# Retention weights split early into two stored parts, and small products on two column tiles

## What is computed

```python
def ab_mixer(...):
    ql, kl, vl, gl, ul = jnp.split(h_lat @ w_in, cuts, axis=-1)   # retention q, k, v, gate; S5 input
    qc, kc, vc, gc, uc = jnp.split(h_ctx @ w_in, cuts, axis=-1)
    r_l, r_c = retention_mixer(...)     # bidirectional retention, 4 heads of 128
    s_l, s_c = s5_mixer(...)            # bidirectional diagonal state space, 32 groups of 16 channels
    y_l = jnp.concatenate([r_l, s_l], axis=-1) @ w_out
```

## Time and profile before

| | |
|---|---|
| Time, median of 3 runs | 1839.15 us (1837.81 to 1839.74) |
| The profiled execution | 1839.42 us, its span 1837.6 us |
| PE busy | 1773.7 us, 97% of the span |
| DVE busy | 1194.3 us, 65% |
| ACT busy | 726.1 us, 40% |
| Moved by DMA | 257.81 MB, 140 GB/s in the mean |
| Granted TensorE clock, mean | 0.987 |

### The profile page before, as it was taken

How to read it: one execution, slowest core, us unless ns; L and a number is a source line. 1 busy time by engine, 2 the same in 40 slices (tenths; PEclk the granted TensorE clock), 3 DMA queues, 4 the chain that set the end, 5 groups by cost and what they waited for, 6 DMA issues and landing times.

```text
span 1837.6 us, 25748 instructions
## 1 busy us (share of the span) xinstructions
PE 1773.7 (97%) x9970; PEld 1516.5 (83%) x9970; DVE 1194.3 (65%) x1890; ACT 726.1 (40%) x1027; POOL 62.2 (3%) x41
## 2 busy tenths in 40 slices
PE   7999999999989799999999999999999999999998
PEld 5788888888787588888888888888888898689997
DVE  4677677778999655876677367766433534855554
ACT  4422122336888734322222242222222433854343
POOL 0000000020000010000000100000002000010001
PEclk8999999999999899999999999999999999999999
DMA  8444454332110122554454335544222342035543
GB/s 333 184 184 154 170 225 183 131 114 74 56 36 35 46 92 100 198 186 163 170 213 147 105 138 190 187 154 177 93 87 96 137 183 69 1 131 183 188 176 124
DMA packets 40440, 257.81 MB, mean 140 GB/s; under 512 B 4752, under 2 KB 6032, under 8 KB 15536
## 3 DMA queue, kind: packets, MB, share of 16 engines
q1 hardware_dynamic: 40368, 256.86, 38.4%
HBM read 255.79 MB, written 1.05 MB: 140 GB/s over the span
## 4 chain that ended last, share of the span: by engine, by line
PE 82%; DVE 10%; ACT 5%; issue 2%; DMA 1%; POOL 0%; ACTq 0%; SPq 0%; DVEq 0%; POOLq 0%
PE ps_all L1796 25%; PE ps_all L1800 25%; PE ps_all L1797 25%; DVE w_lo L1048 2%; ACT w_hi L568 2%; DVE sq_acc L1526 1%; PE ps_all L1792 1%; PE banks L2359 1%; PE banks L2172 1%; PE ps_all L2336 1%; DVE normed L1535 0%; PE ps_all L2159 0%; DVE scaled L1517 0%; DVE wb L1490 0%; PE banks L1891 0%
## 5 line engine op out<-in xcount | busy, mean ns | idle before, releaser
L1796 PE MATMUL ps_all<-a_hi,w_lo 128*128 128x512 f32 (+1 forms) x1832 | 650.9, 355 | 5.0 <-DVE gated L1086 1.6
L1800 PE MATMUL ps_all<-a_lo,w_hi 128*128 128x512 f32 (+1 forms) x1832 | 646.8, 353 | 2.1 <-DVE a_lo L1202 1.2
L1797 PE MATMUL ps_all<-a_hi,w_hi 128*128 128x512 f32 (+1 forms) x1832 | 645.7, 352 | 0.0
L1048 DVE TENSOR_TENSOR w_lo<-w_raw,w_hi 128x2048 fp32r<-128x2048 f32 (+2 forms) x179 | 365.0, 2039 | 149.6 <-ACT w_hi L568 149.4
L568 ACT ACTIVATE w_hi<-w_raw 128x2048 fp32r<-128x2048 f32 (+2 forms) x179 | 306.1, 1710 | 318.3 <-PE ps_all L1800 307.6
L1796 PEld LDWEIGHTS ps_all<-a_hi,w_lo 128*128 128x128 f32 x1832 | 345.9, 189 | 56.2 <-DVE w_lo L1048 4.2
L1800 PEld LDWEIGHTS ps_all<-a_lo,w_hi 128*128 128x128 f32 x1832 | 345.9, 189 | 51.5 <-DVE a_lo L1202 2.7
L1797 PEld LDWEIGHTS ps_all<-a_hi,w_hi 128*128 128x128 f32 x1832 | 346.0, 189 | 47.1 <-issue 0.2
L1060 DVE SCALAR_TENSOR_TENSOR mod_junk<-mod_raw,cond 128x1024 bf16<-128x1024 f32 x256 | 302.7, 1220 | 7.7 <-ACT cond L596 5.4
L1796 PE MATMUL ps_all<-g_hi,w_lo 128*128 128x512 f32 (+1 forms) x734 | 261.2, 356 | 1.5 <-DVE w_lo L1048 1.5
L1797 PE MATMUL ps_all<-g_hi,w_hi 128*128 128x512 f32 (+1 forms) x734 | 259.3, 353 | 0.0
(11 more groups left out here) (280 smaller groups left out, 1526.4 us busy)
## 6 DMA issues: line engine op xcount, KB each, us to landing
w_raw<-in_tiles SPq DMA_DIRECT2D x118, 1024.0 KB, 4.8
mod_raw<-in_w_mod SPq DMA_DIRECT2D x64, 1024.0 KB, 4.8
w_raw<-in_tiles SPq DMA_DIRECT2D x32, 768.0 KB, 4.1
w_raw<-in_tiles SPq DMA_DIRECT2D x32, 640.0 KB, 3.8
start_w<-in_w_start SPq DMA_DIRECT2D x8, 1024.0 KB, 19.3
bias<-in_na_bias SPq DMA_DIRECT2D x2, 1536.0 KB, 9.2
h<-in_h SPq DMA_DIRECT2D x4, 512.0 KB, 7.0
cond<-in_cond SPq DMA_DIRECT2D x2, 1024.0 KB, 18.0
```

Of the source, the lines that this page charges most:

```text
L1048: nc.vector.tensor_tensor(w_lo[:, slot, 0:size], w_raw[:, slot, 0:size], w_hi[:, slot, 0:size].bitcast(F32), ALU.subtract).then_inc(lo_rea ...
L1796: pe.matmul(dst, w[1], x[0], start=start, stop=False)
L1797: pe.matmul(dst, w[0], x[0], start=False, stop=False)
L1800: return pe.matmul(dst, w[0], x[1], start=False, stop=stop_)
```

## The change

The retention tiles are no longer split in the mixer. A new input `split` holds them as 16 pieces of 128 x 1024. In `ffn0.up0` from tile 2 on, and in the first six tiles of `ffn0.down0`, SP loads one piece per tile, ACT rounds it (`piece_to_high`, behind silu and `g_hi`), DVE subtracts (`piece_to_low`, behind gating or residual), and SP stores both parts in a tensor `parts` in device memory. Round 1 of `ffn0.up0` is taken out of the loop on SP, ACT and DVE. In the mixer SP loads `parts` straight into `w_hi` and `w_lo` (`fetch_parts`), and PE waits for `parts_in` in place of `lo_ready`. The glu tiles are loaded earlier, and semaphore counts are adapted. The kernel products of both pairs of a round are issued alternately on two column tiles (PSUM partitions 0 to 31 and 32 to 63).

```diff
+        def piece_at(segment, it, slot):
+
+            if segment == "ffn0.up0" and not early(it, 1):
+                return 2 * it + slot - 2
+            if segment == "ffn0.down0" and not (isinstance(it, int) and it == 3):
+                return 2 * it + slot + 10
+            return None
+
+        piece_raw = scaled[:].rearrange("p s t -> p (s t)")
+        piece_high = normed[:].rearrange("p s t -> p (s t)").bitcast(F32R)
+        piece_low = sq[:].rearrange("p s t -> p (s t)").bitcast(F32R)
...
+            def store_piece(p):
+
+                sp.wait_ge(piece_hi, p + 1)
+                sp.dma_start(parts[bass.ds(p, 1), 0].rearrange("a p c -> (a p) c"), piece_high.bitcast(F32)).then_inc(piece_stored, 16)
+                sp.wait_ge(piece_lo, p + 1)
+                sp.dma_start(parts[bass.ds(p, 1), 1].rearrange("a p c -> (a p) c"), piece_low.bitcast(F32)).then_inc(piece_stored, 16)
+
+            def load_piece(p):
+
+                if early(p, 1):
+                    sp.wait_ge(a_ready, KT)
+                src = i["split"][bass.ds(p, 1)].rearrange("a p c -> (a p) c")
+                sp.dma_start(piece_raw, src).then_inc(piece_in, 16)
+
+            def fetch_parts(j):
+
+                sp.wait_ge(pe_done, BASE["ret_in"] + j - 1)
+                sp.dma_start(w_hi[:, j % 2].bitcast(F32).rearrange("p (a c) -> p a c", a=2),
+                             parts[2 * j:2 * j + 2, 0].rearrange("a p c -> p a c")).then_inc(parts_in[j % 2], 16)
+                sp.dma_start(w_lo[:, j % 2].bitcast(F32).rearrange("p (a c) -> p a c", a=2),
+                             parts[2 * j:2 * j + 2, 1].rearrange("a p c -> p a c")).then_inc(parts_in[j % 2], 16)
+
+            def retention_input():
+
+                for j in range(1, 8):
+                    fetch_parts(j)
+                    if j <= 2:
+                        sp.wait_ge(lo_ready, BASE["ret_in"])
+                        sp.dma_start(w_raw[:, j - 1, 0:width("glu")], i["tiles"][BASE["glu"] + j - 1, :, 0:width("glu")]
+                                     ).then_inc(w_in[j - 1], 16)
+
             def body(segment, it, last):
 
                 for slot in range(2):
                     n = BASE[segment] + 2 * it + slot
+                    if segment == "s5_in" and slot == 1:
+                        sp.wait_ge(piece_stored, 32 * PIECES)
+                        fetch_parts(0)
+                        continue
+                    if segment == "glu" and slot == 0:
+                        continue
                     if early(n, 1):
...
                     fetch_mod(segment, it, slot)
+                    p = piece_at(segment, it, slot)
+                    if p is not None:
+                        if not early(p, 1):
+                            store_piece(p - 1)
+                        load_piece(p)
+                    elif segment == "ffn0.down0" and slot == 0:
+                        store_piece(PIECES - 1)
...
+                if segment == "ffn0.up0":
+                    body(segment, 1, False)
                 if its > 2:
-                    with sp.Fori(1, its - 1) as it:
+                    with sp.Fori(2 if segment == "ffn0.up0" else 1, its - 1) as it:
                         body(segment, it, False)
...
+            def piece_to_high(p):
+
+                if p is not None:
+                    act.wait_ge(piece_in, 16 * (p + 1))
+                    if early(p, 1):
+                        act.wait_ge(a_ready, KT)
+                    else:
+                        act.wait_ge(piece_stored, 32 * p)
+                    nc.scalar.activation(piece_high, piece_raw, ACT.Copy).then_inc(piece_hi, 1)
...
                         finish(it, slot)
+                        piece_to_high(piece_at(segment, it, slot))
...
-                split_hi(base + 1, 2048, 1)
...
-                    split_hi(base + b + 2, 2048 if b < 6 else width("glu"), b % 2)
+                    if b >= 6:
+                        passed[0] = 64
+                        split_hi(base + b + 2, width("glu"), b % 2, 9 if b == 6 else 1)
...
+            def piece_to_low(p):
+
+                if p is not None:
+                    dve.wait_ge(piece_hi, p + 1)
+                    if not early(p, 1):
+                        dve.wait_ge(piece_stored, 32 * p)
+                    nc.vector.tensor_tensor(piece_low, piece_raw, piece_high.bitcast(F32), ALU.subtract).then_inc(piece_lo, 1)
...
                         gating(it, slot)
+                        piece_to_low(piece_at(segment, it, slot))
...
-                    if b < 7:
-                        split_lo(base + b + 2, 2048 if b < 6 else width("glu"), b % 2)
+                    if b == 6:
+                        split_lo(base + 8, width("glu"), 0, 9)
...
-                        pe.wait_ge(lo_ready, n + 1)
+                        pe.wait_ge(parts_in[slot], 32 * (j // 2 + 1))
...
-                def kernel_products(pair):
-
-                    b, ql = pair // 2, pair % 2
-                    at = 224 * ql
+                def kernel_products(b):
+
                     pe.wait_ge(S["c"], b + 1)
                     pe.wait_ge(S["present"], b + 1)
                     if b:
                         pe.wait_ge(S["k"], 2 * b)
-                    c = [cp[:, b % 2, ql, ri] for ri in range(2)]
-                    fwd = [wb[:, 2 * ql, ri, 3, :] for ri in range(2)]
-                    bwd = [wb[:, 2 * ql + 1, ri, 0, :] for ri in range(2)]
+                    c = [[cp[:, b % 2, ql, ri] for ri in range(2)] for ql in range(2)]
+                    fwd = [[wb[:, 2 * ql, ri, 3, :] for ri in range(2)] for ql in range(2)]
+                    bwd = [[wb[:, 2 * ql + 1, ri, 0, :] for ri in range(2)] for ql in range(2)]
+                    to = [ps_sum[32 * ql:32 * ql + 32] for ql in range(2)]
                     for ri in range(2):
-                        pe.matmul(ps_sum[0:32, at:at + 96], bwd[ri], state_rows(c[ri][:, 6:9]), start=(ri == 0), stop=(ri == 1))
-                    pe.matmul(ps_sum[0:32, at + 96:at + 224], fwd[0], state_rows(c[0][:, 0:4]), start=True, stop=False)
-                    pe.matmul(ps_sum[0:32, at + 96:at + 224], fwd[1], state_rows(c[1][:, 0:4]), start=False, stop=False)
+                        for ql in range(2):
+                            pe.matmul(to[ql][:, 0:96], bwd[ql][ri], state_rows(c[ql][ri][:, 6:9]), start=(ri == 0), stop=(ri == 1))
                     for ri in range(2):
-                        pe.matmul(ps_sum[0:32, at + 96:at + 128], bwd[ri], c[ri][:, 9, :], start=False, stop=False)
-                    pe.matmul(ps_sum[0:32, at + 96:at + 128], const[0:32, C_IDENT:C_IDENT + 32], skip[:, pair, :],
-                              start=False, stop=True).then_inc(S["kmm"], 1)
+                        for ql in range(2):
+                            pe.matmul(to[ql][:, 96:224], fwd[ql][ri], state_rows(c[ql][ri][:, 0:4]), start=(ri == 0), stop=False)
+                    for ri in range(2):
+                        for ql in range(2):
+                            pe.matmul(to[ql][:, 96:128], bwd[ql][ri], c[ql][ri][:, 9, :], start=False, stop=False)
+                    for ql in range(2):
+                        pe.matmul(to[ql][:, 96:128], const[0:32, C_IDENT:C_IDENT + 32], skip[:, 2 * b + ql, :],
+                                  start=False, stop=True).then_inc(S["kmm"], 1)
...
-                        kernel_products(2 * b + 2)
-                        kernel_products(2 * b + 3)
+                        kernel_products(b + 1)
```

More of the change, by code:

```diff
@@ L73 @@
 BIAS_BESIDE = ("na_q", "na_v")
+PIECES = 16
 C_BIAS, C_GAIN, C_GLU, C_COND = 0, 2 * CHUNKS, 2 * CHUNKS + 56, 2 * CHUNKS + 60
@@ L165, in laid_out @@
          (np.arange(P)[:, None] % 32 == np.arange(2)).astype(np.float32)], 1)
+    out["split"] = (out["tiles"][BASE["ret_in"]:BASE["ret_in"] + 8].reshape(8, P, 2, 1024).transpose(0, 2, 1, 3)
+                    .reshape(PIECES, P, 1024))
     out["w_mod"] = (x["w_mod"].transpose(0, 2, 1).reshape(UNITS_MOD, 2, P, D).transpose(0, 2, 1, 3)
@@ L192, in program @@
 def program(nc, i, out):
+    parts = nc.dram_tensor("parts", (PIECES, 2, P, 1024), F32, kind="Internal").ap()
     with ExitStack() as ctx:
@@ L541, in _ @@
                 mixer_loads(sp, segment)
+                if segment == "ret_in":
+                    retention_input()
+                    continue
                 its = SIZE[segment] // 2
@@ L596, in up @@
                         nc.scalar.activation(cond[:], cond[:], ACT.Silu).then_inc(cond_ready, 1)
-                with act.Fori(1 if opens else 0, SIZE[segment] // 2 - 1) as it:
+                if segment == "ffn0.up0":
+                    body(1, False)
+                with act.Fori(2 if segment == "ffn0.up0" else 1 if opens else 0, SIZE[segment] // 2 - 1) as it:
                     body(it, False)
@@ L639, in down @@
                 elif "down" in segment:
-                    step(0, 0, True)
-                    step(1, 1)
+                    for slot in range(2):
```

(11 more changed lines are left out.)

24 lines of the change are left out of this document (15 added, 9 removed).

## The result

The changed kernel took 1844.3 us, the median of 8 runs (1842.11 to 1845.77), beside 1838.51 us before (8 runs, 1837.35 to 1839.92): a ratio of 1.0026, with a 95% interval from 1.0016 to 1.0037. So it is 5.8 us slower, just past what can be told from no change. The forecast was 1839.6 us. Both sums behind it were off, and in the same direction.

What follows compares the result with a forecast made beforehand. PE carries 82% of the chain, with DVE setting mixer rounds 0 to 3 and a DVE-ACT loop the others. 1839.42 + 13.3 (first block) - 12.8 (mixer) - 0.3 = 1839.6 us; own range 1836 to 1843, range given 1833 to 1850.

Steps and rivals of the forecast that it cites:

- Both sums: Whole kernel: first block loses 13.3 us (8.3 + 5.0), mixer gains 12.8 us (8.8 + 4.5 - 0.55).
- Waits at tiles 15, 17 and 19: First block's down tiles: PE waits 1.7 us three times because mod loads queue behind a store; 5.0 us lost.
- rival (c): Tile 13, first block: the new 3.4 us wait lowers PE's clock, costing some 3 us; 1842.9 us if none absorbed; chance 0.12.
- Later ones absorb the rest: Down tiles: clock loss at tile 13 counted 0, as the next split is 1.7 us late anyway and later ones absorb.
- A gap of 1.74 shows none: Trace before: a PE gap of 1.74 us shows no clock fall, where one of 3.14 us does.
- The landing 9.2 us after the low half: Down tiles: mod load, queued behind a store waiting for DVE's low piece (194.9 for the first), lands at 204.1.
- Rival (b): First block: stores occupy DMA engines 2.3 times as long as loads, up rounds become 12.05 us; 1849.5 us; chance 0.18.
- The removed splits: Mixer rounds 0 to 5: 2.21 us saved in each of rounds 0 to 3 (8.8), and 4.5 us in rounds 4 and 5.
- The column tiles: Pair loop: fourteen small products take 1.2 us instead of 2.36; worth nothing in rounds 0 to 3, up to 1.8 in 4 and 5.
- The first tile: First retention tile, mixer: its parts land about 432.0, PE starts it at 430.46 now; cost 0.55 us.
- PE's own work there is 19.56 us, so it follows: Mixer rounds 0 to 3: PE's work fits under DVE's 20.15 us, so rounds shorten by 2.21 each, 8.8 us.
- own sign of being wrong: Wrong if up tiles stay at 10.9 us, mod loads gate DVE there, or PE or ACT keeps rounds above 20 us.

Runs made afterwards that it cites:

- tile0_split: Changed kernel, but the first retention tile is loaded whole and split by ACT and DVE as before the change; 1840.46 us against 1839.77.
- best_qk_first: `up_pieces_tile0` with ACT's evacuation of qk moved ahead of the odd pair's scan_rates in rounds 0 to 4; 1823.38 us (0.9922).
- small_down_stores: Changed kernel, but the twelve stores of the down pieces move 128 x 32 values each in place of 128 x 1024; 1844.12 us (1.0027).
- mod_load_first: Changed kernel, but the mod loads of tiles 14, 16 and 18 are issued one tile earlier, ahead of the waiting stores; 1846.63 us (1.0044).
- up_pieces_tile0: Changed kernel with pieces only in ffn0.up0 and ffn0.up1, low half, stores and loads reordered, first retention tile split, unit-8 wait removed; 1826.7 us against 1839.77.
- sp_and_dve_order: Changed kernel with piece stores and loads issued one tile later and DVE's low half behind the next tile's split; 1859.5 us (1.0104).
- no_down_pieces: Changed kernel without the six pieces of the down tiles, leaving ten in ffn0.up0; 1839.6 us against 1838.89 (1.0002).
- pieces_only: Mixer of the kernel before, plus the changed kernel's pieces in the first block, stored but unused; 1853.74 us (1.0075).
- mixer_only: Changed kernel's mixer with no pieces in the first block, parts holding other numbers; 1831.4 us against 1838.88 (0.9952).

## Why the prediction came out as it did

**First block.** The order of events was as forecast, down to the tile. The up round: 11.5 us (11.44). Gating 3 came 2.1 us late (2.7). PE late at the second down tile: 187.57 + 2.20 - 181.84 = 7.9 us (8.3), its wait 3.3 (3.4). Waits at tiles 15, 17 and 19: 1.73, 1.69 and 2.15 us (1.7 each). (The sum's own arithmetic has two small slips that change nothing: gating 11 comes to 181.07 and not 181.04, and three times 1.7 is 5.1.)

What the sum lacked stands behind the waits. From one wait to the next PE falls back by 2.0, 2.0 and 2.4 us: the bracketed time leaves out the tail of the product ahead of it (0.16 us), and the first product behind it takes 0.34 us in place of 0.227. And the clock falls after the last, which with that first product takes the loss from 14.3 to 16.1.

So the step of the first block that failed is the price of the clock. The prediction looked for it at tile 13 alone, as rival (c), and counted nothing behind the waits at tiles 15 to 19, of which nothing absorbs the last. At tile 13 a fall is about as likely as not: of the eight traces with a wait of 2.9 to 3.4 us there, four show the clock at 0.5 behind it. But with the down pieces in place that loss is absorbed, as the prediction had it. The three such traces with the fall have a B - A of 349.7, 350.4 and 351.9 us, and the four without it 350.0 to 354.3.

"Later ones absorb the rest" held. "A gap of 1.74 shows none" held for that gap, but it was no bound: 2.15 and 2.18 us were enough, in `tile0_split` 1.80 at tile 19, and in `best_qk_first` 1.31 behind a gap of 0.93.

**The mod loads.** The landing 9.2 us after the low half came out at 9.5. That is no proof of its terms: without the store's 0.5 MB the same sum (0.5 MB at 420 GB/s) gives 1.2 us less, and `small_down_stores` shows 9.1 to 10.5. The traces are mixed on why the mod load is late: not for the stores' bytes (`small_down_stores`, where the engines are all the same 81 to 99% busy while it is under way); and issuing them earlier helps the mod data only, since then the piece's load is late (`mod_load_first`). My reading is that with one buffer for the piece and one for the mod data a load can be issued only when DVE is done. It takes 5 to 9 us, and the round is 8.2, so two such chains on one queue don't both fit. No run with a second buffer tests this, and the cause stays open as far as that goes.

Rival (b) did not come. No row gave its factor of 2.3. The up tiles of `up_pieces_tile0` keep their 10.88 us with the same five transfers (DMA share 0.92 from 97.37 to 151.77 us, 338 GB/s), and a store of 0.5 MB lands in 2.7 and 3.0 us in the median, a load in 4.7 (in the down tiles 3.6 and 3.9 against 5.1). The Trainium skill, DMA: Bandwidth & Descriptors, "Where 436 GB/s comes from", has about 358 GB/s as one core's HBM limit; the window 240 to 242 us of the trace after, with loads and stores, moved 436 GB/s, so the trace doesn't agree.

**Mixer.** The removed splits gave 2.21 us in each of rounds 2 and 3, and rounds 4 and 5 came to 17.97 us (17.95 and 18.15). The column tiles: fourteen products from 461.02 to 462.21, 1.19 us (1.2). Their worth was right in size by luck: 1.19 us in rounds 4 and 5 (up to 1.8), and 1.13 in round 0 (0). The first tile: with the 14.0 us taken off by which B comes later, PE started at 446.26 - 14.0 = 432.26 (432.0), and the state products came 0.8 us later than before (0.55). The step that failed is "PE's own work there is 19.56 us, so it follows". A round isn't set by the largest of the engines' own sums, as ACT sits between PE and DVE. In round 0 DVE waits for `tcos`, which waits for PE's `turn_w` (0.74 us), and PE waits 2.18 us for ACT's `qk`, after which the clock fell (1.09 us). The prediction's own sign of being wrong, a round above 20 us because PE took DVE's place, came true in round 0.

**Sum.** Forecast 13.3 - 12.8 = 0.5 us; by the marks 16.2 - 10.9 = 5.3; measured 5.8. Of the 4.8 us missing, 2.7 are clock (1.6 in the first block, 1.1 in the mixer), and 0.7 are round 0. The measured 1844.3 us lies inside the stated range and above the forecast's own 1836 to 1843, and no rival had this mechanism at its price. Rival (c), 1842.9, came nearest, with the right cause at the wrong tile.

## What to carry to other kernels

Work moved off a full engine costs what its place costs: the same 16 pieces cost 14 to 16 us behind the gating and in the down tiles, and nothing by the trace between two products that DVE can do anyway, in segments with a round of 10.9 us. When an instruction waits for another engine, move it to where its input is already there; moved behind the split it held its buffer too long, and the up tiles of `sp_and_dve_order` stayed at 11.4 to 11.5 us. When a buffer has one copy, add up issue, landing and use around the whole loop, and not only bytes over bandwidth. In an estimate for a kernel like this one, a wait of PE of some 2 us should be carried at its length plus 1 to 3 us, with a chance near one half, and not at its length alone: the fall came in four of eight traces at tile 13, and in six of ten with the wait of 2.18 us for `qk`.

## What the runs showed of the hardware

The clock doesn't follow from the length of the wait before it:

```
kernel            wait of PE     granted clock after
after             3.33 us        1.00
no_down_pieces    3.36           0.50 for about 6 us, same tile
pieces_only       2.89           0.61 (188 to 192), same tile
after             2.35           1.00
mixer_only        2.65           0.50, same place
after             2.18           0.50
up_pieces_tile0   2.18           1.00, same place
after             2.15           0.52
tile0_split       1.80           0.50 (244 to 246)
best_qk_first     1.31           0.50 (524 to 526)
```

In `best_qk_first` PE had been busy 1.8 of the 4 us from 520 to 524, in pieces. In `no_down_pieces` the clock is down as soon as PE goes on, in `mixer_only` about 1.0 us later. A fall costs 1.1 to 3.1 us. The Trainium skill, TensorE: Matmul & The Clock Gate, "What's actually happening", says that the chip's observation of activity runs on its own clock and not with the kernel; these pairs agree. It means that one profiled execution shows one draw, and that terms of this kind belong in the range. It also bounds these comparisons: in the pairs above, kernels with the same or nearly the same wait differed by 1.1 and 1.6 us in a stage for this reason alone.
